# Two layers of gated linear attention, one core: split projections in the first layer, level work shared with GpSimd in the fourth

## The reference

```python
# layer 1: gated linear attention, 4 heads, key width 96, value width 192
proj = h @ w_in                      # q 384, k 384, v 768, g_low 16, q_mem 256, gate 1024
log_a = log_sigmoid(g_low @ w_gate_up + b_gate) / 16
...                                  # chunks of 64 tokens, a state per head
# layer 2: dilated attention; layers 1 and 2 also attend to 256 memory tokens
# layers 3 and 4 (second_block, l = 0 and 1): modulated norms, then a mixer with
#   a two-way gated scan (4 heads of width 128), differential attention, a Fourier mix; then a SwiGLU
ml = silu(c) @ w_mod[l] + b_mod[l]   # 1024 x 6144 per layer, for two conditions
o_t = q_t S_t,  S_t = diag(f_t) S_{t-1} + k_t^T v_t
```

## Time and profile before

| | us |
|---|---|
| median of 3 runs | 3282.18 (3277.76 to 3287.8) |
| profiled execution | 3282.0 |
| its span, first to last instruction | 3280.7 |
| PE busy | 2975.9 (91%) |
| DVE busy | 1602.5 (49%) |
| ACT busy | 1011.7 (31%) |
| POOL busy | 99.6 (3%) |

### The profile page before, as it was taken

One profiled execution on the slowest core, in us unless ns is written; L12 is line 12 of the kernel. 1 busy time (PEld: TensorE's weight loads), 2 busy tenths in 40 slices (PEclk: granted clock), 3 DMA queues, 4 the chain that ended last, 5 costly groups with the idle time before them and its releaser, 6 DMA issues.

```text
span 3280.7 us, 44026 instructions
## 1 busy us (share of the span) xinstructions
PE 2975.9 (91%) x18450; PEld 2399.2 (73%) x18450; DVE 1602.5 (49%) x3473; ACT 1011.7 (31%) x1950; POOL 99.6 (3%) x46
## 2 busy tenths in 40 slices
PE   6988899999999999888699999999899797799998
PEld 4657688889977666677568888888666686578886
DVE  3122445444446255676863433334825667645354
ACT  2011432233343155243232211212426344232222
POOL 0000000000000100100000000000210000000001
PEclk9999899999999999799899999999999798799999
DMA  5423231222222110222522111121120010222321
GB/s 184 150 94 129 84 115 48 58 59 66 71 96 103 52 33 1 81 78 78 168 77 90 52 64 65 52 78 65 39 60 18 17 40 14 90 90 85 108 88 66
DMA packets 227299, 246.61 MB, mean 75 GB/s; under 512 B 5553, under 2 KB 193053, under 8 KB 225565
## 3 DMA queue, kind: packets, MB, share of 16 engines
q1 hardware_dynamic: 227100, 243.79, 23.1%
HBM read 234.34 MB, written 9.44 MB: 74 GB/s over the span
## 4 chain that ended last, share of the span: by engine, by line
PE 55%; DVE 10%; ACT 3%; issue 2%; DMA 1%; POOL 0%; ACTq 0%; DVEq 0%; POOLq 0%; SPq 0%
PE PS L2049 51%; PE PS L2053 2%; PE PS L2258 2%; DVE AR L2780 1%; ACT AR L174 1%; DVE AR L2768 1%; DVE AR L2769 1%; DVE AR L3020 1%; ACT L169 1%; DVE STAT L2956 1%; DVE AR L2789 0%; DVE EX L3007 0%; ACT EX L174 0%; DMA WR<-in_w_in 0%; ACT STAT L174 0%
## 5 line engine op out<-in xcount | busy, mean ns | idle before, releaser
L2049 PE MATMUL PS<-HI,WC 128*128 128x512 f32 (+2 forms) x1600 | 428.2, 353 | 0.6 <-DVE WC L3001 0.6
L2049 PE MATMUL PS<-AR 128*64 128x64 f32 (+8 forms) x3756 | 319.1, 269 | 64.5 <-ACT AR L174 22.2
L2049 PE MATMUL PS<-WR,HT 128*128 128x256 f32 (+2 forms) x1744 | 363.7, 367 | 10.9 <-ACT AR L174 6.8
L2049 PE MATMUL PS<-HT,WR 128*128 128x256 f32 (+3 forms) x1136 | 348.9, 461 | 21.2 <-ACT EX L174 5.7
L2049 PEld LDWEIGHTS PS<-AR 128*64 128x64 f32 (+5 forms) x3756 | 274.8, 173 | 116.6 <-issue 42.2
L2049 PE MATMUL PS<-DW,DH 128*128 128x384 f32 (+1 forms) x1344 | 355.7, 347 | 0.9 <-DVE AR L2631 0.9
L174 ACT ACTIVATE AR<-PS 128x256 f32<-128x256 f32 (+3 forms) x389 | 165.5, 452 | 614.6 <-PE PS L2049 470.1
L2049 PEld LDWEIGHTS PS<-WR,HT 128*128 128x128 f32 x1744 | 281.9, 199 | 76.7 <-issue 42.7
L2049 PEld LDWEIGHTS PS<-HI,WC 128*128 128x128 f32 x1600 | 284.1, 189 | 42.4 <-DVE WC L3001 1.1
L2049 PEld LDWEIGHTS PS<-HT,WR 128*128 128x128 f32 (+2 forms) x1136 | 210.2, 190 | 127.3 <-issue 88.1
L2049 PE MATMUL PS<-LO,WC 128*128 128x512 f32 (+2 forms) x800 | 282.5, 353 | 0.0
(11 more groups left out here) (345 smaller groups left out, 4339.7 us busy)
## 6 DMA issues: line engine op xcount, KB each, us to landing
WR<-in_w_ffn_in SPq DMA_DIRECT2D x40, 1024.0 KB, 7.4
WR<-in_w_in_b SPq DMA_DIRECT2D x51, 512.0 KB, 5.9
WR<-in_w_mod SPq DMA_DIRECT2D x12, 2048.0 KB, 8.1
WR<-in_w_mod SPq DMA_DIRECT2D x24, 1024.0 KB, 5.3
WR<-in_w_ffn_out SPq DMA_DIRECT2D x22, 1024.0 KB, 4.9
WR<-in_w_in SPq DMA_DIRECT2D x40, 512.0 KB, 4.2
WR<-in_w_out SPq DMA_DIRECT2D x8, 2048.0 KB, 9.5
WR<-in_w_in_a SPq DMA_DIRECT2D x8, 1024.0 KB, 5.3
```

The costliest lines, as they stand in the source:

```text
L2049: mm = lambda o, l, r, start, stop: e.o.matmul(o, l, r, start=start, stop=stop, skip_group_check=True)
```

## The change

In layer 1, the 13 pieces of `w_in` are multiplied as three fp32r products. The tokens' norm writes a high half `HA` where `HT` was (columns 0 to 511) and a low half `LA` over `X`, so X is loaded again from memory after the last token projection (`x0`), and the out projection waits for it. `SplitPiece` makes the halves of a piece in four groups of two k rows: a cvh on ACT and a cvl on DVE each, the low half in place of the raw slab, the high half in one of two buffers. `ahead` converts groups of the next piece: two after each `features`, one after each tile of `tokens`. A third raw buffer `q1` (upper half of buffer 1) lets loads run two pieces ahead. The modulation stream of this stage has 24 chunks of 256 columns (1 MB) in the lower half of buffer 1, 7 yields a chunk, at 4.5 steps a yield (3 in the end) instead of 1.4 (1).

In layer 4 alone, `hl1` and `hl2` are cut in two: DVE keeps the query side (7 of the 14 subtracts; 7 products of 128x128 instead of 128x256) and POOL does the key side (7 subtracts, 7 products of 128x128 a unit). ACT's Exp waits for both, and so do the products `hl3`.

```diff
+        beside_mods = wslots["q1"]
+        wslots["q1"] = WR[:, 6144:8192]
+        HA, LA = at("HA", HT_AT, 6144, F32R).rearrange("p (k n) -> p k n", k=8), at("LA", X_AT, 4096, F32R).rearrange("p (i k n) -> p i k n", i=4, k=8)
-                fetched.append(load(ap, 8, n, ("q0", "q2")[len(fetched) % 2]))
+                fetched.append(load(ap, 8, n, ("q0", "q2", "q1")[len(fetched) % 3]))
+            def convert(self, groups):
+                for j in self.left[:groups]:
+                    ks = slice(2 * j, 2 * j + 2)
+                    m = P.add("cvh", self.his[j], self.chunk.view[:, ks, :], self.chunk.ready, self.until)
+                    m = P.add("cvl", self.his[j], self.lo[:, ks, :], self.chunk.view[:, ks, :], m)
+                    self.ready = Chunk(self.chunk.slot, None, ("cv_d", m), (), ())
+        def split_piece():
+            w = splits[-1]
+            w.convert(4)
+            piece()
+            next_split()
+            return w
-        mods = modulation(0, MODH, 7, [1] * 12)
+        mods = modulation(0, MODH, 7, [1] * 24, width=256)
-        items += [Norm(X3[:, i, :], [HT3], 128 * i, vec("norm"), None, [(f"x{i // 2}", 16)]) for i in range(4)]
+        items += [Norm(X3[:, i, :], [HA, LA[:, i]], 128 * i, vec("norm"), None, [(f"x{i // 2}", 16)]) for i in range(4)]
         def features(w, c0, m, dst, eng, scale=None):
-            yield from steps_of(lambda bk: bk[0:m, 0:512], [(w.view[:, k, c0:c0 + m], hk(k)[:, 0:512]) for k in range(8)], w, ths[5], dst, eng, scale)
+            pairs = []
+            for k in range(8):
+                wh, wl = (a[:, c0:c0 + m] for a in (w.his[k // 2][:, k % 2, :], w.lo[:, k, :]))
+                pairs += [(wh, HA[:, k, 0:512]), (wl, HA[:, k, 0:512]), (wh, LA[:, :, k, :])]
+            yield from steps_of(lambda bk: bk[0:m, 0:512], pairs, w.ready, ths[5], dst, eng, scale)
+            ahead(2)
         def tokens(dst, eng, free=()):
...
+                    pairs += [(h, wh), (h, wl), (lw, wh)]
+                yield from steps_of(lambda bk: bk[:, 0:256], pairs, w.ready, ths[5], dst(i), eng(i), None, free, halves=False)
+                ahead(1)
+            w.used()
+            P.add("ld", "x0", X3, A["x"].rearrange("o (i p) n -> p (o i) n", p=128), 0, (("pj", P.count["pj1"]),))
-        for _ in with_some(with_some(projections(), lanes, LANES), mods, 1.4, 5):
+        for _ in with_some(with_some(projections(), lanes, LANES), mods, 4.5, 5):
```

DVE's `hl1` and `hl2`, where `shared` is set in layer 4:

```diff
-                    tt(x4[:, :, tk, :], ref, b4[:, :, tk, :], ALU.subtract)
+                    if not shared:
+                        tt(x4[:, :, tk, :], ref, b4[:, :, tk, :], ALU.subtract)
                     s = tt(x4[:, :, tq, :], b4[:, :, tq, :], ref, ALU.subtract)
+                    if shared:
+                        v = lambda a: a.rearrange("p (n t h) -> p n t h", t=2, h=h)[:, :, 0 if rev else 1, :]
+                        m = tt(v(x3[:, l, :]), v(x3[:, l, :]), v(H.q[:, 128 * i:128 * i + 256]), ALU.mult)
+                        continue
```

POOL's new `hl1` and `hl2`:

```diff
+            def hl1(n, H, i, d, xb, until, shared):
...
+                e.wait_ge(*H.cum[d])
+                e.wait_all(until)
+                for l in range(7):
...
+                    s = tt(v(x3[:, l, :])[:, :, 1 if rev else 0, :], ref.broadcast_to([K, 128 // h, h]), b4[:, :, 1 if rev else 0, :], ALU.subtract)
+                s.then_inc(sem("hl_g"))
+            def hl2(n, H, i, d, L, shared):
...
+                e.wait_ge(*L["exped"])
+                for l in range(7):
+                    v = lambda a: a.rearrange("p (n t h) -> p n t h", t=2, h=64 >> l)[:, :, 1 if rev else 0, :]
+                    m = tt(v(x3[:, l, :]), v(x3[:, l, :]), v(k[:, 128 * i:128 * i + 256]), ALU.mult)
+                m.then_inc(sem("hl_g"))
```

More of the change, by code:

```diff
@@ L729, in piece, with __init__, used, ahead @@
             return fetched[taken[0] - 1]
+        class SplitPiece:
+            def __init__(self, p, chunk):
+                n = chunk.view.shape[2]
+                his = ([AR_AT + 4 * (24896 + 512 * j) for j in range(4)], [AR_AT + 4 * (26944 + 512 * j) for j in range(3)] + [XC_AT + 4 * 1536])[p % 2]
+                raw = {"q0": WR_AT, "q2": WR_AT + 4 * 2048, "q1": WR_AT + 4 * 6144}[chunk.slot]
+                self.p, self.chunk, self.left, self.until = p, chunk, list(range(4)), split_until[p % 2]
+                self.his = [at(f"WA{p}h{j}", a, 2 * n, F32R).rearrange("p (k n) -> p k n", k=2) for j, a in enumerate(his)]
+                self.lo = k3(at(f"WA{p}l", raw, 8 * n, F32R), 8)
+            def convert(self, groups):
[4 more added lines that the diff above has]
+                    self.ready = Chunk(self.chunk.slot, None, ("cv_d", m), (), ())
+                del self.left[:groups]
+            def used(self):
+                split_until[self.p % 2] = (("pj", P.count["pj1"]),)
+        split_until, splits = [(), ()], []
+        def ahead(groups):
+            if splits[-1:] and splits[-1].left:
+                splits[-1].convert(groups)
+        def next_split():
+            if len(splits) < 13 and taken[0] < len(fetched):
+                splits.append(SplitPiece(len(splits), fetched[taken[0]]))
+        def split_piece():
[4 more added lines that the diff above has]
+            return w
+        fetch()
         fetch()
@@ L801, in projections @@
             P.add("setup2")
-            yield from features(piece(), 0, 16, GL[0:16, :], "d")
+            next_split()
+            w = split_piece()
+            yield from features(w, 0, 16, GL[0:16, :], "d")
+            w.used()
             ready = got[-1:]
@@ L808, in projections @@
                 known["lg", h] = [("gl_l", n)]
+                ahead(1)
                 yield
-            n, w = len(got), piece()
+            n, w = len(got), split_piece()
             for f in range(2):
                 yield from features(w, 128 * f, 128, QM1[:, f, :], eng_of(f))
+            w.used()
             known["qm"] = since(n)
@@ L1116, in units @@
             return [(i, d) for i in H.outs[::2] for d in range(len(H.dirs))]
+        shared_levels = itertools.count(1)
         def levels_begin(H, u):
@@ L1120, in levels_begin @@
             j, xb, until = H.b["X"].take()
-            n = P.add("hl1", H, i, d, xb, until)
+            shared = None if H.alone else next(shared_levels)
+            n = P.add("hl1", H, i, d, xb, until, shared)
             H.lv[u] = dict(j=j, xb=xb, exped=("hl_e", n))
@@ L1126, in levels_weigh @@
             i, d = H.units[u]
-            n = H.weighed = P.add("hl2", H, i, d, H.lv[u])
-            H.lv[u]["weighed"] = [("hl_w", n)]
+            shared = None if H.alone else next(shared_levels)
+            n = P.add("hl2", H, i, d, H.lv[u], shared)
+            H.lv[u]["weighed"] = H.weighed = [("hl_w", n)] if H.alone else [("hl_w", n), ("hl_g", shared)]
         def levels_multiply(H, u):
@@ L1625, in build @@
                          [VH[:, i, :] for i in range(6)], list(range(nt)), hb[h % 2], hpair, hturn if h else prr, hout)
+                H.alone = both
                 H.beside = [KQ, KQ[:, 768:3840]]
@@ L2753, in hp5, with hl1 @@
                     stt(s3[:, nx, :], s3[:, i, :], H.dec[d][0:H.K, i:i + 1], r, ALU.mult, ALU.add).then_inc(sem("hp_u"))
-            def hl1(n, H, i, d, xb, until):
+            def hl1(n, H, i, d, xb, until, shared):
                 k, lg, rev, order = H.dirs[d]
@@ L3051, in rj @@
                 tt(o, a, b, ALU.add).then_inc(sem("rj"))
-            return dict(fence=fence, rj=rj, hp2=hp2, g2=g2, an=an, dump=dumped(e))
+            return dict(fence=fence, rj=rj, hp2=hp2, hl1=hl1, hl2=hl2, g2=g2, an=an, dump=dumped(e))
         def sp_program(e):
```

43 lines of the change are left out of this document (33 added, 10 removed).

## The result

| | before | after |
|---|---|---|
| median, us | 3280.36 (3277.76 to 3287.8) | 3303.98 (3301.34 to 3304.34) |
| profiled execution, its span | 3282.0, 3280.7 | 3303.8, 3302.5 |
| layer 1 ends (PE at the fence) | 347.2 | 378.1 |
| layer 4, before the scan + scan | 188.3 + 225.5 | 185.9 + 220.2 |
| all other stages | 2519.7 | 2518.3 |

The changed kernel is slower, by a ratio of 1.0068 [1.0056, 1.0079]. That is 16 us more than forecast. But the sum hides two larger misses. Layer 1 lost 30.9 us where 3 were to be gained, and layer 4 gained 7.7 where 9 were to be lost: +33.9 - 16.7, and -1.4 elsewhere.

The account below looks back on a forecast made before the run. PE, busy 91% of the span, was taken to bound the kernel, with DVE's chain setting the end of layer 4's scan. Layer 1's -3 and layer 4's +9 us on 3282.0 gave 3288 us, range 3258 to 3314.

Parts of the forecast that it names:

- The products: Layer 1's projections of x: three products of halves replace eight float32 ones, 31.7 us less on PE, all on the path.
- The features' boundaries: Layer 1, five piece changes in `features`: PE waits for eviction and the next piece's conversions, 2.3 or 2.8 us each, 12.5 us.
- The tokens' boundaries: Layer 1, behind `tokens`: PE waits for the one conversion group left, 1.4 us six times, 8.4 us; all boundaries together 0 to 30.
- The first piece: Layer 1, before the first product: the last x tile's norm adds an ACT copy and a DVE subtract, 1.4 us.
- The lanes' steps: Layer 1: shorter tiles cover less of the lanes' waits for DVE and ACT, and conversions stand ahead: 3 us, bounds 0 to 8.
- The gate steps' chunks: Layer 1's short gate steps: three half-size modulation chunks instead of two waits, one 3.87 us, the other about as long; sum set equal.
- The late chunks: Layer 1, later modulation: three chunks each follow the one before by a single tile, 3 to 4 us, bounds -4 to 12.
- Layer 4: Shared levels: DVE and POOL exclude each other, end rounds grow from 8.0 to some 10.2 us; +9 us, bounds -14 to +35.
- a freer DVE: Rival, layer 4: small DVE and POOL operations slip between each other, end rounds fall to 5.6 us and a hop; 3265, chance 0.11.
- The middle of layer 4: Scan from 2600 to 2765 us: levels asked for a unit ahead, PE has projections; 0, bounds -6 to +22.
- The rival of the shared port: Layer 4's middle: DVE steps wait for whole POOL strings, PE's work queues behind, 20 us more; 3308 us, chance 0.27.
- rivals of late chunks: Layer 1: every modulation chunk late by 1 us in 20 places, with PE's clock dropping; 3303 us, chance 0.06.

## Why the prediction was right in its total and wrong in its parts

- **The products** (-31.7 us): near at full clock. Records of 512 columns stand 0.23 us apart, 0.69 a triple. A tile of 24 records of 256 columns takes 3.13 us where 16 float32 ones took 3.62 to 3.72, and a group of 24 of 512 columns 5.8 us where it was 7.1. That makes some 29 us, as each group still ends with its last record's way out. (The sum itself has a small slip: eight products at 0.43 us a record take 6.9 us and not 7.0, and 88 x 0.18 is 15.8.) Wrong as a gain on the path: only 9.3 us of busy time went.
- **The features' boundaries** (12.5 us): 11.5 measured, in the five places named, ended by the line named. What was missing is their second price. Taking the boundaries of both kinds away gave 15.7 us of idle time and 9.3 of busy time. My sum had no term for the granted clock in layer 1, though the earlier trace rows show it fall where PE's work is thin, and I had counted 29 us of new idle time in that very stretch. This is the step that failed most: some 13 of 34 us.
- **The tokens' boundaries** (8.4 us): 0.6, 2.3 and 1.9 at three and under 0.4 at the others, some 5 in all. Too high by 3.
- **The first piece** (1.4 us for the norm's end): 9.16 us, where before had 0.99: a miss of 6.8 us, the second largest. The step that failed is the placing. I priced the two operations I saw added, and not that in a plan replayed in order they stand behind `setup2`, which the product had not depended on until it needed a conversion on those engines. With `setup2` behind, 3.16 us are left, of which the conversions themselves are about 1.
- **The loads' order**: the second load ahead of the constants moved the first product by 2.85 us. I had not costed it. It turned out to be worth nothing at the fence, though the lead had stood for 100 us.
- **The lanes' steps** (3 us): 5.0. PE's idle time ahead of them rose from 24.3 to 29.3 us.
- **The gate steps' chunks** (set equal, 7.4 us): 10.7 us, in three waits instead of two, and the half clock from 63.5 to 87.4 us lies over them. The reading was wrong as well. The profile names no releaser for the 3.87 us of the earlier trace rows, and its chunk had landed at 49.5 us: PE waited for the clearing of the bank. So 3.5 us of waiting for chunks became 5.4, and 3.9 us for the clearing became 5.3. The late chunks (3.4 us) were about right: 4.8 us in five places, 1.71 at the longest.
- **Layer 4** (+9 us): -7.7. The durations were right (POOL's 0.4 us; its strings take 2.6 us where least disturbed, 0.37 an operation; POOL busy 106 us more). What failed is the round, 10.2 us forecast and 6.0 and 8.2 measured, in two steps. First, I took from the earlier trace rows, where one POOL product of 1.9 us held a DVE operation, that strings of seven hold each other. In the runs the engines alternate operation by operation: the first five of DVE's operations in the string at 2832.84 us start every 0.4 us, and between each two of them one of POOL's starts. The three pairs of strings in these rounds take 4.5, 3.4 and 3.9 us from the first start to the last end, hardly less than 1.5 + 2.6 one behind the other, but DVE never stands still for a whole string. The Trainium skill (SBUF — State Buffer, Who interferes with whom) has the lock held for one instruction; the trace agrees, and seven in a row are seven chances to get in. Second, I put POOL's strings, DVE's and the Exp in a row. In the round of 8.2 us DVE works without a gap, 3.2 + 2.5 us on its stretched strings and 2.6 on `hl4`, and the Exp lies beside `hl4`; in the round of 6.0 POOL's part was done ahead and DVE's strings ran alone. The rival "a freer DVE" named the mechanism; its size, -14 us, was too much, since DVE's subtractions grew from 0.28 to 0.40 us and the halved multiplications took as long as the whole ones had.
- **The middle of layer 4** (0): right, 164.3 and 164.4 us. The rival of the shared port did not come there. A loss of its kind did come in layer 3, once the levels were shared there.
- **The total**: 3304 lies in the range and on the side given most chance, but by luck: a miss of +34 and one of -17 partly cancel. It lies nearest to the rivals of late chunks (3303) and of the shared port (3308), and neither mechanism made it. Of the signs to look for, the triples, the five waits and the times of POOL and DVE came, of the six tokens' waits three; the rounds of 10 us did not, and they carried the term with the wrong sign.

## What to carry to other kernels

Cheaper products gain only if what makes their operands is planned ahead of where PE will be: put each conversion beside the product before the last one, not behind it, and look for what unrelated work (a table load, a setup chain) stands ahead of it on the same queue. New idle time in a stretch that PE filled must be costed twice, once as itself and once through the clock it takes from the work around it; here 2 us between pieces cost some 3. A releaser that the profile does not name has to be looked up in the plan before it is priced. And work given to a second engine that shares a port pays by the operation: take what is whole and small off the busy one, and don't halve an operation whose half, beside the other engine, takes as long as the whole did.

## What the runs showed of the hardware that was not expected

- Seven DVE operations of 128x128 take 1.50 us alone and 2.5 to 3.2 us beside seven of POOL, which take 2.9 to 3.6 then; neither waits for the other's whole string.
- A multiplication of 128x128 beside POOL takes DVE 434 ns (layer 4) to 512 ns (layer 3) in the mean, and one of 128x256 without POOL's share 441 to 456.
- The same products with 16.1 us less idle time between them took 7.7 us less busy time, with the clock at half for 14.3 us less in layer 1.
- Three us gained at the start were gone 200 us later, with the half clock's stretches lying elsewhere and 7 us longer. And the same 16 records at the start of the same code took 3.7 to 6.7 us from one execution to the next: single microseconds in such a stretch can't be read off at one place.
